# Windowed attention over a narrower set of keys, with latent tokens ordered by grid column

## The chip, the cores and the metric

The kernel runs on 1 core of one Trainium2 chip. The metric is the device time of one execution in microseconds (us); the time before is the median of 3 runs.

## The reference

Two trunk layers act on 640 tokens of width 1024: 512 latent tokens, which lie on a grid of 8 rows by 64 columns, and 128 context tokens. Each layer applies a modulated RMSNorm, one combined q/k/v projection, attention in three groups of heads, an output projection, a second norm, and an expert layer (for each token 8 heads choose 16 of 16384 single-neuron experts). What the change touches is group A, six heads of neighbourhood attention:

```
col_ok = (kcols >= cs_b) & (kcols < cs_b + NA_COLS)        # a window of 16 columns per query
bias = rpb[:, dr_idx][:, :, dc_idx]                        # learned, by row and column distance
s_lat = einsum(q_row, k_blk) * scale + bias
s_lat = where(mask, s_lat, -inf)
s_ctx = einsum(q_row, k_ctx) * scale                       # all 128 cached context keys
p = softmax(concatenate([s_lat, s_ctx]))
o = einsum(p[..., :nk], v_blk) + einsum(p[..., nk:], v_ctx)
```

The window is min(8, rows) rows high, which here is all 8 rows, and 16 columns wide, clamped at the edges: the first column of the window is clip(column - 8, 0, 48). Groups B (4 heads, two softmax maps each) and C (6 query heads on 2 key heads) attend to all latent and all context keys. Context queries see context keys alone.

## The kernel before, in words

Everything stays in SBUF apart from the weights, which stream through a ring of four 512 KB blocks by SyncE's queue (lines 372 to 400), and the experts. Tokens lie in 5 tiles of 128: tiles 0 to 3 are latent, tile 4 is context. A latent tile holds two grid rows, since token = 64 * row + column.

The stages are: modulation from `w_mod` (for layer 0 at the very start, 48 blocks, `mod_tile`, L460), norm, projection, attention, output projection, norm, queries, experts. The two expert stages gather 1280 times in all (5 tiles of 128 slots in each layer), 128 rows of 8 KB each time, by GpSimd's queue (L1310). VectorE takes the dot products (L1252), ScalarE builds a diagonal (L858 to L868), TensorE adds up (L660).

**Attention** (`attention(l)` on each engine) works through the list MAPS, made by `attention_plan`: first group A (3 chunks of 2 heads, each over tiles 0 to 4: 30 maps, 24 of them latent), then B (40 maps), then C (30 maps). A map is one head's softmax over one tile of queries. Per pair of maps:

- TensorE computes the scores of both, 512 latent keys in one matmul (L547), 128 cached context keys in a second (L549), into two PSUM pairs. A context tile has one matmul of 128 keys (L544). It first waits for the exponentials of the pair before, since the two PSUM areas are used again.
- VectorE adds the bias table to the 512 latent scores in PSUM (L1086, group A alone), and takes the negated row maximum over 640 columns (L1087); after the exponential it takes the reciprocal of the sum (L1092).
- ScalarE takes the exponential of 640 columns with its sum (L772) into one of 8 `prob` buffers.
- GpSimd multiplies by the reciprocal (L1346).
- Three maps later TensorE transposes the probabilities, 5 blocks of 128 (L579), and ScalarE copies them from PSUM (L782). Four maps later TensorE multiplies them with the values, 5 blocks for two heads (L564), and ScalarE copies the result (L787).

A float32 matmul shows as two instructions in the trace, so x4 of L547 is two score tiles, x20 of L564 is 5 blocks of 2 heads. Each engine's order is written out by hand in its loop over n; TensorE's is scores of a pair, then values of a unit, then transposes of an item.

**The bias table** is 6 heads by 896 columns on 128 partitions. GpSimd's queue loads it at the head of each layer behind the rotary tables and the cached keys and values (L1319 to L1325), as two DMAs of 64 partitions, each reading 14 of 15 rows of 64 values for each head. Then GpSimd adds the column mask in 6 instructions of 896 columns (L1329). In layer 0 this stands beside the modulation blocks, in layer 1 beside the first norm, where VectorE writes the normed activations (`norm`, L1020, L1022, L1027). VectorE waits for `bias_ready` only at the head of attention.

## Time and profile before

| | us |
|---|---|
| median of 3 runs (lowest, highest) | 5093.67 (5089.64, 5100.22) |
| the profiled execution, its own time | 5083.82 |
| its span, first to last instruction | 5082.0 |
| layer 0: attention, from the last projection tile to the last copy | 318 to 632 |
| layer 1: the same | 2827 to 3141 |

The profile gives one execution: for each engine the busy time, for each idle stretch what ended it, and the chain of work that ended last. PEclk is TensorE's granted clock as a share of full speed (0.50 is the lower of its two levels, 1.2 GHz, and 1.00 the upper, 2.4 GHz). Matmul durations double, nearly, from the one to the other.

### The profile page before, as it was taken

Reading aid. Unit: us, or ns where it says so; the run is one execution under the profiler, and the core shown is the slowest. Engines: PE = TensorE matmul, PEld = TensorE weight load, DVE = VectorE, ACT = ScalarE, POOL = GpSimd, SP = SyncE. Lnnn points to the kernel's source line nnn. Section 1 sums busy time; section 2 is a strip of 40 time slices with the busy share of each in tenths; the row PEclk is TensorE's granted clock in tenths of the full one; section 3 lists DMA queues with packets and bytes.
Section 4 is the critical chain, followed back from the end, with each engine's and each line's share of the span. In section 5 each row is a group of like instructions: output and inputs, shape, how many; then the busy total and the mean of one; then the engine's idle time right before and its main releaser. Section 6 shows DMA issues by size and latency. Waiting matters only on the chain.

```text
span 5082.0 us, 42863 instructions
## 1 busy us (share of the span) xinstructions
PE 3751.2 (74%) x14332; PEld 1733.4 (34%) x14332; DVE 2830.4 (56%) x6026; ACT 1445.8 (28%) x4223; POOL 1400.0 (28%) x1477
## 2 busy tenths in 40 slices
PE   5777779777777777777767776867777777777776
PEld 1464435222222222323234544442222222222222
DVE  2443365564675756754455334557657567576544
ACT  1223422222222222222222334222222222322222
POOL 1011200233343333433320111003333434334332
PEclk8886789899999999999988858989999999999999
DMA  8110012999999999999951000119999999999997
GB/s 277 54 36 1 1 58 91 392 410 414 417 413 420 415 408 410 409 411 380 419 188 47 19 1 14 62 55 410 418 415 412 415 416 409 419 409 416 417 420 294
DMA packets 214077, 1460.21 MB, mean 287 GB/s; under 512 B 23968, under 2 KB 24224, under 8 KB 49248
## 3 DMA queue, kind: packets, MB, share of 16 engines
q0 software_dynamic: 186496, 1355.11, 65.2%
q1 hardware_dynamic: 27360, 102.37, 5.8%
q8 instruction: 113, 1.85, 0.1%
q14 instruction: 108, 0.88, 0.0%
HBM read 1453.19 MB, written 4.19 MB: 287 GB/s over the span
## 4 chain that ended last, share of the span: by engine, by line
PE 39%; DMA 38%; DVE 12%; ACT 6%; issue 4%; POOL 0%; SPq 0%; ACTq 0%; DVEq 0%; POOLq 0%
DMA work<-expert_dram,work 26%; PE psum L660 17%; DMA hT<-expert_dram,work 10%; PE psum L449 10%; DVE work L1252 4%; PE psum L547 3%; PE psum L564 2%; PE psum L579 2%; ACT work L868 2%; PE psum L519 2%; DVE hT L1252 2%; DVE work L992 1%; ACT work L858 1%; DMA ring<-w_mod_dram 1%; ACT work L782 1%
## 5 line engine op out<-in xcount | busy, mean ns | idle before, releaser
L660 PE MATMUL psum<-work 128*128 128x512 f32 x3416 | 1611.7, 616 | 560.3 <-ACT work L868 554.9
L1252 DVE SCALAR_TENSOR_TENSOR work<-work,psum 128x1024 f32<-128x1024 f32 x854 | 1041.5, 1220 | 875.8 <-DMA work<-expert_dram,work 875.4
L1310 POOL DMA_INDIRECT work<-expert_dram,work x854 | 831.6, 974 | 1522.6 <-PE psum L660 1349.9
L660 PEld LDWEIGHTS psum<-work 128*128 128x128 f32 x3416 | 627.9, 193 | 1534.2 <-ACT work L868 885.1
L660 PE MATMUL psum<-hT,work 128*128 128x512 f32 x1704 | 805.7, 617 | 317.7 <-ACT work L868 317.2
L858 ACT ACTIVATE work<-work,xinv 128x2 f32<-128x2 f32 x640 | 189.1, 295 | 2385.2 <-DVE work L1252 1588.6
L1252 DVE SCALAR_TENSOR_TENSOR hT<-hT,psum 128x1024 f32<-128x1024 f32 x426 | 519.5, 1220 | 428.5 <-DMA hT<-expert_dram,work 428.3
L1310 POOL DMA_INDIRECT hT<-expert_dram,work x426 | 413.0, 969 | 834.4 <-PE psum L660 668.4
L660 PEld LDWEIGHTS psum<-hT,work 128*128 128x128 f32 x1704 | 312.8, 193 | 803.4 <-ACT work L868 485.5
L449 PE MATMUL psum<-hT,split 128*128 128x128 f16 (+1 forms) x2880 | 436.2, 313 | 58.3 <-DVE hT L1027 58.3
L868 ACT ACTIVATE work<-const,work 128x128 f32<-128x128 f32 x1280 | 434.1, 386 | 0.0
L449 PEld LDWEIGHTS psum<-hT,split 128*128 128x128 f16 x2880 | 233.2, 101 | 265.0 <-issue 71.7
L862 ACT ACTIVATE work<-work 128x1 f32<-128x1 f32 x1280 | 307.1, 287 | 20.8
L1087 DVE TENSOR_REDUCE stat<-psum 128x1 f32<-128x640 f32 (+1 forms) x200 | 141.0, 710 | 266.5 <-PE psum L549 209.0
L941 DVE SCALAR_TENSOR_TENSOR split<-ring,bscale,split 128x1024 f16<-128x1024 f32 x88 | 112.8, 1282 | 201.0 <-ACT split L701 200.4
L564 PE MATMUL psum<-work 128*64 128x128 f32 x1344 | 122.5, 342 | 122.8 <-ACT work L782 122.8
L772 ACT ACTIVATE work<-psum,stat 128x640 f32<-128x640 f32 (+1 forms) x200 | 141.7, 708 | 239.5 <-DVE stat L1087 238.7
L547 PE MATMUL psum<-work 64*128 64x512 f32 (+1 forms) x320 | 142.6, 983 | 50.3 <-ACT work L772 47.9
L1346 POOL TENSOR_SCALAR work<-work,stat 128x640 f32<-128x640 f32 (+1 forms) x120 | 85.2, 713 | 284.6 <-DVE stat L1092 284.6
L460 PE MATMUL psum<-ring,cT 128*2 128x512 f32 x384 | 107.4, 660 | 58.0 <-DMA ring<-w_mod_dram 49.5
L579 PE MATMUL psum<-const,work 128*128 128x128 f32 x672 | 141.6, 349 | 8.2 <-ACT work L782 8.2
L564 PEld LDWEIGHTS psum<-work 128*64 128x64 f32 x1344 | 97.1, 173 | 145.2 <-ACT work L782 145.2
(152 smaller groups left out, 2744.5 us busy)
## 6 DMA issues: line engine op xcount, KB each, us to landing
ring<-w_mod_dram SPq DMA_DIRECT2D x96, 512.0 KB, 5.6
ring<-w_in_dram SPq DMA_DIRECT2D x40, 512.0 KB, 3.5
ring<-w_query_dram SPq DMA_DIRECT2D x32, 512.0 KB, 3.6
work<-expert_dram,work POOLq DMA_INDIRECT x854, 8.5
ring<-w_out_dram SPq DMA_DIRECT2D x16, 512.0 KB, 3.5
hT<-expert_dram,work POOLq DMA_INDIRECT x426
work<-rpb_dram POOLq DMA_DIRECT2D x4, 1344.0 KB, 19.2
xT<-xT_dram SPq DMA_DIRECT2D x1, 2560.0 KB, 11.7
```

The lines of the kernel that those rows point to most:

```text
L449: last = pe.matmul(out[:, lo:hi_], w[:, i, k, :], x[:, j, k, lo:hi_], start=(s == 0 and n == 0), stop=(s == KC - 1 and n == 2))
L547: pe.matmul(ps[:, 0:NLAT], q, qk[kp:kp + kn, m["k"], 0:NLAT], start=True, stop=True)
L564: last = pe.matmul(psum[64 * hh:64 * hh + 64, 6 + u % 2, 0:P], v, probT[:, u % 2, hh, b * P:(b + 1) * P], start=(b == 0), stop=(b == nb - 1))
L579: last = pe.transpose(pair[2][:, b * P:(b + 1) * P], src[:, b * P:(b + 1) * P], con("ident"))
L660: last = pe.matmul(out[:, cols_], diag[:, n % NDIAG, :], rows[n % NBUF][:, D + 512 * half:D + 512 * half + 512], start=(s == 0), stop=(s = ...
L772: act.activation(prob[:, n % NPROB, 0:w], pair[n % 2][:, 0:w], ACT.Exp, bias=stat[:, 0, n % NPROB:n % NPROB + 1], accum_out=stat[:, 1, n % ...
L858: act.activation(act_out[:, s:s + 2], act_in[:, s:s + 2], ACT.Gelu_apprx_tanh, scale=xinv[:]).then_inc(gelu_done, 1)
L862: act.activation(coef[:, s + k:s + k + 1], act_out[:, s + k:s + k + 1], ACT.Copy, scale=weight[:, t % 2, s + k:s + k + 1]).then_inc(coef_d ...
L868: act.activation(diag[:, (n + k) % NDIAG, :], con("ident"), ACT.Copy, scale=coef[:, s + k:s + k + 1]).then_inc(diag_done, 1)
L1087: dve.tensor_reduce(stat[:, 0, n % NPROB:n % NPROB + 1], ps[:, 0:TOK if lat else NCTX], AX_X, ALU.max, negate=True).then_inc(max_done, 1)
L1252: dve.scalar_tensor_tensor(u, u, 1.0, pair[t % 2], ALU.mult, ALU.mult, accum_out=act_in[:, s:s + 1]).then_inc(dot_done, 1)
L1310: pool.indirect_dma_start(rows[n % NBUF], None, a[f"expert{l}"], bass.IndirectOffsetOnAxis(expert[:, t % 2, s:s + 1], 0)).then_inc(row_in[ ...
```

## The change

The latent tokens are put in the order 8 * column + row, so that a tile of 128 queries is 16 columns of all 8 rows, and a range of keys is a range of columns. The host orders the input, the rotary tables and the output accordingly. For group A the table COL_SPAN gives for each latent tile the first latent key, the number of latent keys and where its columns start in the bias table: 256 keys for tiles 0 and 3, 384 for tiles 1 and 2. Scores, bias add, maximum, exponential, scaling, transposes and the product with the values work on these keys and the 128 of context alone. The bias table is laid out on the host as 896 columns for each head (256 + 384 + 256, of which tiles 1 and 2 use the same 384), and loaded by one DMA of 128 partitions with 5376 values in a row; the mask is 112 columns, each added to 8 neighbouring values. Groups B and C have the same work as before.

```diff
+COL_SPAN = ((0, 256, 0), (0, 384, 256), (128, 384, 256), (256, 256, 640))
...
-          ("iota", 128), ("iota16", 16), ("mask", 64)]
+          ("iota", 128), ("iota16", 16), ("mask", 112)]
...
+def span(m):
+
+    if m["t"] == TT - 1:
+        return NLAT, 0
+    return COL_SPAN[m["t"]][0:2] if m["kind"] == "A" else (0, NLAT)
+
+
+def width(m):
+    return span(m)[1] + NCTX
...
-        bias = at(o, 6, BROWS, GRID_W); o += 6 * BROWS * GRID_W
+        bias = at(o, 6, 896); o += 6 * 896
...
-                                    pe.matmul(ps[:, 0:NLAT], q, qk[kp:kp + kn, m["k"], 0:NLAT], start=True, stop=True)
+                                    at_, nk = span(m)
+                                    pe.matmul(ps[:, 0:nk], q, qk[kp:kp + kn, m["k"], at_:at_ + nk], start=True, stop=True)
...
-                                    last[x] = pe.matmul(ps[:, NLAT:TOK], q, kc[kp:kp + kn, m["cc"], :], start=True,
+                                    nk = span(m)[1]
+                                    last[x] = pe.matmul(ps[:, nk:nk + NCTX], q, kc[kp:kp + kn, m["cc"], :], start=True,
...
-                        nb = TT if it["t"] < TT - 1 else 1
+                        nb = width(it) // P
...
-                                v = vN[:, TT - 1 if nb == 1 else b, vs] if b < TT - 1 else vc[:, vs]
+                                v = vc[:, vs] if nb > 1 and b == nb - 1 else vN[:, span(it)[0] // P + b, vs]
...
-                        for b in range(TT if it["t"] < TT - 1 else 1):
+                        for b in range(width(it) // P):
...
-                        w = TOK if m["t"] < TT - 1 else NCTX
+                        w = width(m)
...
-                            r0 = 6 - 2 * m["t"]
-                            b = bias[:, m["head"], r0:r0 + ROWS, :].rearrange("p r c -> p (r c)")
-                            link(dve.tensor_tensor(ps[:, 0:NLAT], ps[:, 0:NLAT], b, ALU.add))
-                        dve.tensor_reduce(stat[:, 0, n % NPROB:n % NPROB + 1], ps[:, 0:TOK if lat else NCTX], AX_X, ALU.max,
+                            nk, at_ = COL_SPAN[m["t"]][1:3]
+                            b = bias[:, m["head"], at_:at_ + nk]
+                            link(dve.tensor_tensor(ps[:, 0:nk], ps[:, 0:nk], b, ALU.add))
+                        dve.tensor_reduce(stat[:, 0, n % NPROB:n % NPROB + 1], ps[:, 0:width(m)], AX_X, ALU.max,
...
-                for par in range(2):
-                    pool.dma_start(bias[64 * par:64 * par + 64],
-                                   a["rpb"][l, :, :, 1 - par:1 - par + BROWS, :]).then_inc(bias_in, 16)
-                pool.wait_ge(bias_in, 16 * 2 * (l + 1))
+                pool.dma_start(bias, a["rpb"][l]).then_inc(bias_in, 16)
+                pool.wait_ge(bias_in, 16 * (l + 1))
                 for h in range(6):
-                    pool.tensor_tensor(bias[:, h], bias[:, h], con("mask").unsqueeze(1).to_broadcast(
-                        [P, BROWS, 64]), ALU.add).then_inc(bias_ready, 1)
+                    b = bias[:, h].rearrange("p (c r) -> p c r", r=ROWS)
+                    pool.tensor_tensor(b, b, con("mask").unsqueeze(2).to_broadcast([P, 112, ROWS]),
+                                       ALU.add).then_inc(bias_ready, 1)
```

## Rows read from the trace of the kernel before

**Rows 1.** The page: DMA share, in tenths, in 40 equal slices of 127 us.
```profile
DMA  8110012999999999999951000119999999999997
```

**Rows 2.** Windows over both A phases, each layer's; columns are in the first line.
```profile
core 0: us, PE busy (x) PEld busy (x) DVE busy (x) ACT busy (x) POOL busy (x), PEclk, DMA share, GB/s
...
325.40:427.40 102.00, 67.83 (x449) 45.38 (x449) 39.12 (x84) 40.56 (x98) 20.93 (x29) 0.74 0.00 1
2834.20:2936.20 102.00, 67.93 (x449) 45.41 (x449) 39.05 (x84) 40.54 (x98) 20.92 (x29) 0.74 0.00 1
```

**Rows 3.** The chain by line, 325.43 to 427.4 us, layer 0's A phase.
```profile
by line: PE psum L547 19.5%; PE psum L564 19.2%; DVE stat L1087 13.1%; PE psum L579 12.0%; DVE psum L1086 10.5%; ACT work L782 8.9%; issue 7.0%; ACT work L772 5.2%; PE psum L549 4.3%; DVE stat L1092 0.2%; ACTq L771 0.1%
```

**Rows 4.** Groups by form in the same stretch: busy us, mean ns | idle before.
```profile
L1087 DVE TENSOR_REDUCE stat<-psum 128x1 f32<-128x640 f32 x24 | 19.8, 824 | 0.8
L772 ACT ACTIVATE work<-psum,stat 128x640 f32<-128x640 f32 x24 | 19.0, 794 | 44.0 <-DVE stat L1087 43.6
L1086 DVE TENSOR_TENSOR psum<-psum,work 128x512 f32<-128x512 f32 x24 | 16.6, 690 | 46.5 <-PE psum L549 46.5
L782 ACT ACTIVATE work<-psum 128x640 f32<-128x640 f32 x22 | 15.4, 699 | 19.6 <-PE psum L579 19.6
L772 ACT ACTIVATE work<-psum,stat 128x128 f32<-128x128 f32 x6 | 2.2, 366 | 0.0
L1087 DVE TENSOR_REDUCE stat<-psum 128x1 f32<-128x128 f32 x6 | 1.7, 282 | 11.7 <-PE psum L544 11.7
L782 ACT ACTIVATE work<-psum 128x128 f32<-128x128 f32 x4 | 1.1, 272 | 1.9 <-PE psum L579 1.9
```

**Rows 5.** Timeline of TensorE in layer 0's A phase: start us, us, what.
```profile
336.01 2.08 PE L547 MATMUL psum<-work 64*128 64x512 f32 x4 [2.83 <-ACT work L772]
338.45 1.33 PE L579 MATMUL psum<-const,work 128*128 128x128 f32 x5
341.68 2.40 PE L564 MATMUL psum<-work 128*64 128x128 f32 x20 [1.90 <-ACT work L782]
356.88 1.31 PE L564 MATMUL psum<-work 128*64 128x128 f32 x20 [0.79 <-ACT work L782]
358.12 0.77 PE L579 MATMUL psum<-const,work 128*128 128x128 f32 x5
358.82 1.13 PE L547 MATMUL psum<-work 64*128 64x512 f32 x4
```

**Rows 6.** Windows: the bias load at the start, and in layer 1.
```profile
15.00:35.00 20.00, 5.62 (x12) 0.28 (x12) 0.00 (x0) 0.00 (x0) 0.00 (x0) 0.53 1.03 248
2598.00:2601.00 3.00, 3.00 (x9) 1.64 (x8) 0.00 (x0) 0.95 (x2) 0.00 (x0) 0.62 0.99 406
2602.00:2614.00 12.00, 4.61 (x20) 2.61 (x18) 6.42 (x8) 4.23 (x5) 0.00 (x0) 0.85 1.00 200
```

**Rows 7.** The chain in order of time at the start: start us, us, what.
```profile
14.93 21.84 DMA ring<-w_mod_dram
```

**Rows 8.** Timeline of VectorE and GpSimd after layer 1's bias load.
```profile
2616.18 13.56 POOL L1329 TENSOR_TENSOR work<-work,const 128x896 f32<-128x896 f32 x6 [18.76 <-DMA work<-rpb_dram]
2618.25 2.71 DVE L1027 TENSOR_TENSOR hT<-work,hT 128x640 f16<-128x640 f32 x1
2631.91 0.82 DVE L1027 TENSOR_TENSOR hT<-work,hT 128x640 f16<-128x640 f32 x1
```

**Rows 9.** Windows: the first pairs of A, and part of B, layer 0.
```profile
325.40:342.00 16.60, 7.86 (x30) 4.55 (x32) 9.22 (x18) 5.94 (x13) 3.39 (x5) 0.50 0.00 0
460.00:540.00 80.00, 59.02 (x283) 37.62 (x282) 32.50 (x73) 30.94 (x80) 11.78 (x15) 0.50 0.00 1
```

**Rows 10.** Timeline: ends of the first, fourth and fifth expert tile, layer 0.
```profile
1284.88 1.02 ACT L837 ACTIVATE work<-psum 128x1024 f32<-128x1024 f32 x1
2260.74 1.00 ACT L837 ACTIVATE work<-psum 128x1024 f32<-128x1024 f32 x1
2589.74 1.02 ACT L837 ACTIVATE work<-psum 128x1024 f32<-128x1024 f32 x1 [3.50 <-PE psum L660]
```

More of the change, by code:

```diff
@@ L48 @@
 B_SCALE = 32.0 ** -0.5
-BROWS = 14
+COL_SPAN = ((0, 256, 0), (0, 384, 256), (128, 384, 256), (256, 256, 640))
 HEADS, TOPK, NK = 8, 16, 128
@@ L776, in attention @@
                         i = BY_LAST[n - LAG_T]
-                        w = TOK if ITEMS[i]["t"] < TT - 1 else NCTX
+                        w = width(ITEMS[i])
                         act.wait_ge(tr_done, NITEM * l + i + 1)
@@ L1342, in _ @@
                         m = MAPS[n]
-                        w = TOK if m["t"] < TT - 1 else NCTX
+                        w = width(m)
                         s = n % NPROB
@@ L1352, in _, with bias_columns, by_column, by_row @@
                 gather(l)
+def bias_columns():
+    q0 = np.repeat([0, 16, 48], [32, 48, 32])
+    kcol = np.concatenate([np.arange(32), np.arange(48), 32 + np.arange(32)])
+    return q0[None, :] + np.arange(P)[:, None] // ROWS, kcol[None, :]
+def by_column(x):
+    return x.reshape(ROWS, GRID_W, D).transpose(1, 0, 2).reshape(NLAT, D)
+def by_row(x):
+    return x.reshape(GRID_W, ROWS, D).transpose(1, 0, 2).reshape(NLAT, D)
 def constants():
@@ L1371, in constants @@
     c["iota16"] = np.tile(np.arange(16), (P, 1))
-    qc = p[:, None] % GRID_W
-    kcol = np.arange(GRID_W)[None, :]
-    lo = np.clip(qc - 8, 0, GRID_W - 16)
+    qcol, kcol = bias_columns()
+    lo = np.clip(qcol - 8, 0, GRID_W - 16)
     c["mask"] = np.where((kcol >= lo) & (kcol < lo + 16), 0.0, NEG)
@@ L1381, in constants @@
         inv = (np.float32(10000.0) ** (-(np.arange(q, dtype=np.float32)) / np.float32(q))).astype(np.float32)
-        pos = np.where((d // (dim // 2) == 0)[:, None], (tok // GRID_W)[None, :], (tok % GRID_W)[None, :])
+        pos = np.where((d // (dim // 2) == 0)[:, None], (tok % ROWS)[None, :], (tok // ROWS)[None, :])
         ang = pos.astype(np.float32) * inv[d % q][:, None]
@@ L1411 @@
     ins = {}
-    x = np.concatenate([x_sample.reshape(NLAT, D), x_prompt.reshape(NCTX, D)], 0)
+    x = np.concatenate([by_column(x_sample), x_prompt.reshape(NCTX, D)], 0)
     ins["xT"] = x.T.reshape(KC, P, TOK).transpose(1, 0, 2)
@@ L1434 @@
         ins[f"expert{l}"] = np.concatenate([peer_u[l], peer_v[l]], 1)
-    rpb = np.zeros((L, 6, 15, 127), na_rpb.dtype)
-    rpb[..., 63 - 15:63 + 16] = na_rpb
-    ins["rpb"] = np.stack([rpb[..., 63 - q:127 - q] for q in range(GRID_W)], 1)
+    qcol, kcol = bias_columns()
+    dc = np.repeat(np.clip(kcol - qcol, -15, 15) + 15, ROWS, axis=1)
+    dr = np.tile(np.arange(ROWS), 112)[None, :] - np.arange(P)[:, None] % ROWS + ROWS - 1
+    ins["rpb"] = na_rpb[:, :, dr, dc].transpose(0, 2, 1, 3)
     ck = np.concatenate([cache_c_k.reshape(L, NCTX, P), cache_b_k.reshape(L, NCTX, 2 * P),
@@ L1457 @@
     v = r["out_v"]
-    return (y[NLAT:].reshape(1, NCTX, D), y[:NLAT].reshape(1, NLAT, D),
+    return (y[NLAT:].reshape(1, NCTX, D), by_row(y[:NLAT]).reshape(1, NLAT, D),
             kT[..., 384:].reshape(1, L, NCTX, 6, 64), v[..., 0:384].reshape(1, L, NCTX, 6, 64),
```

## The prediction

> **What bounds the kernel now.** I read the page first, for the shape of the whole. The DMA share stands at nine tenths or more for 25 of 40 slices [rows 1]: these are the two expert stages, where the gathers set the pace. The change leaves their number and size alone. It acts in the slices with a DMA share near nothing, where attention runs, so I cut a window out of each layer, from the first bias add to the first score tile of group B [rows 2]. Both last 102 us, with TensorE busy 68 us, VectorE 39 and ScalarE 41, and a DMA share of 0.00. No engine is full, and nothing hides the phase. The chain through it [rows 3] says why: it hands on from scores (L547, L549) to bias add and maximum (L1086, L1087), exponential (L772), copy (L782), values (L564), transposes (L579), and then to the next scores, which wait for the exponentials of the pair before. "Issue", 7.0%, is mostly the second exponential's own run. A shorter piece of any of them shortens the loop.
>
> **The change, part by part.** A latent tile of group A has 256, 384, 384 and 256 latent keys in place of 512, a mean of 320, so 192 columns fewer, and 448 wide instead of 640 with the context. Values and transposes go from 5 blocks to 3, 4, 4, 3: 1.5 fewer. Context tiles, B and C keep their work. Each term is the part of the 102 us that a line has on the chain [rows 3] times the share that it loses.
>
> Scores, L547: 19.5% or 19.9 us. Four instructions of 512 columns take 2.08 us at the lower clock and 1.13 at the upper [rows 5], the difference 0.95 being 4 x 512 columns at one clock against the other. So the columns are 1.90 us of 2.08, and 192 of 512 of that is 0.71, or 34%. Part of the rest also hides behind the L549 pair, and I take 30%: 6.1 us.
> Values, L564: 19.2%, 19.6 us. x20 takes 2.40 or 1.31 us [rows 5], so columns are 2.18 of 2.40; 6 of 20 instructions fewer is 0.65, 27%; I take 5.0 us.
> Transposes, L579: 12.0%, 12.2 us; 1.33 or 0.77 us for five [rows 5], columns 1.12; 1.5 of 5 is 0.34, 25%; I take 2.8 us.
> Maximum, L1087: 824 ns at 640 columns and 282 at 128 [rows 4], 1.06 ns a column, so 0.20 us or 25% of 13.1% (13.4 us): 3.3 us.
> Bias add, L1086: 690 ns [rows 4], one width only; with the slope of the maximum 0.20 us or 29% of 10.7 us: 3.1 us.
> Exponential, L772: 794 and 366 ns [rows 4], 0.84 ns a column, 0.16 us or 20% of about 10.5 us (5.2% and half of "issue" and more): 2.1 us.
> Copy, L782: 699 and 272 ns [rows 4], 0.16 us or 23% of 9.1 us: 2.1 us.
> Sum: 24.5 us for a layer, 49 us for two, as long as TensorE's clock stays at the 0.74 of both phases. GpSimd's scaling gets shorter too, but is behind the chain (21 us of 102 [rows 2]); I cost it at nothing, and nothing comes to depend on it. What is late next is the same loop: TensorE's fixed wait for two exponentials.
>
> The clock is the open cost of this part. TensorE's work falls by about as much as the loop (at the mean of both clocks some 0.5 us of scores, 0.5 of values and 0.5 of transposes a unit, 12 units: 18 of 68 us, beside 24.5 of 102), so its share goes from 0.67 to 0.65 only. But the first pairs, which have scores and transposes alone and a share of 0.47, ran at 0.50, and so did B with a share of 0.74 [rows 9]. If all of A ran at 0.50, the chain's 11 score tiles would be 11 x 2.08, its 11 value groups 11 x 2.40, transposes and L549 some 21 us: 70 us against 56 now, and after the cut about three quarters of those 14 us, 10.7 us a layer. If all ran at 1.00, it would be some 12 us a layer better. Being half way, and with the share nearly unchanged, I take no correction.
> The Trainium skill ("TensorE: Matmul & The Clock Gate", The HAM clock gate) says that the throttled state is the default and that activity releases it. By that rule less work among waits that stay would speak against this change, and the sum would be nearer that of the lower clock; the first pairs agree with it, B with its share of 0.74 does not.
>
> **The bias table's load.** Its bytes are the same 2.75 MB a layer, but as 128 rows of 21504 bytes, where before each of 64 partitions had pieces of 14 x 256 bytes. It is slow now: in layer 1 the queue moves 406 GB/s while the tables before it run, and 200 GB/s with the DMA engines as full while the bias runs [rows 6]. At the start 20 us pass at 248 GB/s with a share of 1.03 [rows 6], and the chain lies on it: 21.84 us of waiting for modulation blocks [rows 7]. If the new form runs like the tables, the same 4.96 MB take 12.2 us at 406: 8 us gained, all on the chain, as everything after waits for these blocks and then for xT. Bounds: nothing (the rate stays at 200), and 10 us. I take 8, since long rows ran at 406 in the same queue.
> In layer 1 it lands 12 us x (1 - 200 / 406), about 6 us, earlier. That matters: GpSimd's six mask adds run 2616.18 to 2629.7, and beside them VectorE's operations on the chain take 2.71 us where 0.82 is normal [rows 8]. There are six such places of about 1.8 us: 10.8 us lost. Six to seven us earlier, about two of the six adds fall under the reciprocal and before the first normed tile at 2613.3, so I take 2 x 1.8 = 3.6 us. Bounds: nothing, if the reciprocal is blocked as well, and 10.8. The mask's new form (112 columns, each repeated over 8 neighbours) has the same 896 elements; no row shows this form, and I take the 2.1 to 2.3 us of one add now.
> The Trainium skill ("SBUF — State Buffer", SBUF: two separate sides) calls the port that VectorE and GpSimd share an exclusive lock for a whole instruction; the 2.71 us agree with that.
> The larger mask is 24.6 KB more of constants, under 0.1 us at the rates above. Issuing one DMA fewer saves 0.7 us on GpSimd's queue, which waits for the landing anyway.
>
> **Sum.** 49 + 8 + 3.6 = 60.6 us. The profiled execution took 5083.8 us, so its like would take 5023. It is 9.9 us below the median of the runs shown, 5093.7; against the median the forecast is 5033.
>
> **Rivals.**
> *The lower clock.* All of A at 0.50 leaves 24.5 - 10.7 = 13.8 us a layer, 27.6 in all; with the load's 11.6 that is 39, so 5055. For it: the first pairs and B. Against it: the share of 0.65. Chance 0.18.
> *The load is no faster.* The bias is slow for another reason than its pieces, such as going to 64 partitions at a time through one queue behind others. Then 49 us remain: 5045. For it: the trace shows the rate, not the cause. Against it: 406 GB/s in the same queue. Chance 0.13.
> *The mask add becomes slow.* This is the case on the other side. If GpSimd handles runs of 8 poorly, each of its six adds blocks VectorE in layer 1's norm for its whole length. One extra us for an add costs 6 us; from 9.5 us extra, 11.6 us an add, it eats the 57 us of the other terms; at 14 us it is 6 x 11.9 - 57 = 14 us slower, 5108, before what it does to layer 0's norm. For it: only that the form is unknown. Against it: five times the price for as many elements. Chance 0.04.
> *It does not do what it says, or not where it counts.* If the narrower tiles did not shorten the loop, since a fixed wait took the place of each cut, the time would be 5094, or up to 11.6 us less with the load's part. Against it: every piece of the chain scales with columns in these rows. Chance 0.02.
> The expert stages gather other rows together. Four tiles took 1304.9 us, 326 us a tile [rows 10]; the last of them took 329.0, 3 us more than that. No row says that the new mix is better or worse. Ten tiles with such differences of their own add some 5 us of spread both ways.
>
> **How the numbers follow.** The forecast case has 0.63, its time is 5033. About 0.2%, or 10 us, is what a measurement of this kernel can tell from no change. The low end is 49 + 8 + 10.8 = 68 off the median, and 8 more if runs fall like the profiled one: 5018. The high end takes in the lower clock with a few us of spread: 5061. Faster takes all cases but the last two, 0.94; slower 0.04; same 0.02.
>
> **What would show it.** In the changed profile: A's windows of 76 to 78 us with a clock near 0.74; the maximum at 0.55 to 0.69 us; x12 and x16 of L564; xT's load issued some 8 us earlier; fewer than six slow operations of VectorE in layer 1's norm. The prediction is wrong if A's windows stay above 88 us, if the clock falls to 0.50 there, if mask adds last over 4 us each, or if the expert tiles differ by more than 5 us each.

## The result and the profile after

The changed kernel takes 5026.79 us, median of 4 runs (5010.99 to 5032.48), beside 5091.66 (5089.57 to 5100.22) for the kernel before: a ratio of 0.9881, with an interval of 0.9852 to 0.9909. It was timed again in a later comparison: 5020.68 us over 6 runs (4995.43 to 5027.24), ratio 0.9859 [0.9832, 0.9885]. So it is faster by 1.2% to 1.4%, about 65 us. The forecast was 5033. The sum came out right; its parts did not, as this section and the next ones show.

The profiled execution took 5023.02 us, of which the span is 5021.2; before, 5083.82 and 5082.0. Cut at the same events in both traces, the 60.8 us of span went like this (us):

| stretch | before | after | difference |
|---|---|---|---|
| start to layer 0's first VectorE operation of attention | 318.4 | 303.5 | -14.9 |
| layer 0: attention, to its last copy | 314.0 | 295.0 | -19.0 |
| of it A | 102.0 | 85.9 | -16.1 |
| of it C, in which nothing was changed | 89.6 | 86.6 | -3.0 |
| layer 0: out-projection and queries | | | -1.4 |
| layer 0: expert stage | 1682.4 | 1672.8 | -9.6 |
| layer 1: norm and projection | 237.4 | 229.9 | -7.5 |
| layer 1: attention (A again 102.0 to 85.9) | 313.7 | 294.9 | -18.8 |
| layer 1: queries | | | +0.6 |
| layer 1: expert stage | 1630.4 | 1638.7 | +8.3 |
| the end | | | +1.5 |

The windows over the two A phases, with the same events at their ends as in [rows 2]. Columns: stretch, its length, then PE, PEld, DVE, ACT and POOL busy (instructions), the granted clock, the DMA share and GB/s.

```profile
310.56:396.48 85.92, 61.55 (x350) 41.81 (x350) 29.50 (x84) 33.27 (x98) 17.18 (x29) 0.58 0.00 1
2781.70:2867.60 85.90, 61.54 (x349) 41.81 (x349) 29.55 (x84) 33.26 (x98) 17.17 (x29) 0.58 0.00 1
```

TensorE has 99 instructions fewer, 350 for 449, and VectorE and ScalarE as many as before but shorter ones. The third number from the end is the surprise: the granted clock fell from 0.74 to 0.58, that is from half way between the two levels (1.2 and 2.4 GHz) to near the lower. TensorE's busy share did not fall: 61.55 of 85.92 is 0.72, where 67.83 of 102.00 was 0.67. But the share isn't independent of the clock: the same instructions last nearly twice as long at the lower level (sixteen value multiplications 1.97 us below, 1.09 at the upper), so a fallen clock by itself raises it.

The chain through the same stretch by line, to lay beside [rows 3] (scores are L559 and L562 now, values L577, transposes L592, bias add L1099, maximum L1100, exponential L785, copy L795):

```profile
by line: PE psum L577 21.6%; PE psum L559 17.4%; PE psum L592 15.0%; DVE stat L1100 11.1%; DVE psum L1099 8.4%; ACT work L795 7.0%; issue 6.5%; PE psum L562 5.6%; ACT work L785 5.4%; PE psum L555 1.7%; DVE stat L1105 0.2%; ACTq L784 0.1%
```

In us of 85.92: scores 15.0 (before 19.9), values 18.6 (19.6), transposes 12.9 (12.2), maximum 9.5 (13.4), bias add 7.2 (10.7), copy 6.0 (9.1). VectorE's pieces and ScalarE's copy fell by more than a quarter. TensorE's values hardly fell and its transposes rose, though more than a fourth of both is gone: each one that is left takes longer.

The groups by form in that stretch, to lay beside [rows 4]:

```profile
L1100 DVE TENSOR_REDUCE stat<-psum 128x1 f32<-128x512 f32 x12 | 8.3, 691 | 0.4
L785 ACT ACTIVATE work<-psum,stat 128x512 f32<-128x512 f32 x12 | 8.2, 687 | 19.4 <-DVE stat L1100 19.1
L795 ACT ACTIVATE work<-psum 128x512 f32<-128x512 f32 x12 | 7.1, 595 | 13.9 <-PE psum L592 13.8
L785 ACT ACTIVATE work<-psum,stat 128x384 f32<-128x384 f32 x12 | 7.0, 580 | 15.8 <-DVE stat L1100 15.8
L1100 DVE TENSOR_REDUCE stat<-psum 128x1 f32<-128x384 f32 x12 | 6.7, 557 | 0.4
L1099 DVE TENSOR_TENSOR psum<-psum,work 128x384 f32<-128x384 f32 x12 | 6.7, 557 | 19.1 <-PE psum L562 19.1
L1099 DVE TENSOR_TENSOR psum<-psum,work 128x256 f32<-128x256 f32 x12 | 5.1, 424 | 20.4 <-PE psum L562 20.4
```

The maximum takes 691 and 557 ns, a mean of 624, where 824 - 192 x 1.06 = 620 was forecast. The bias add takes 557 and 424, a mean of 490, and 690 - 200 = 490 was forecast from another operation's slope. The exponential's mean is 634 for a forecast of 634. What each narrower instruction costs was known; the slopes held.

TensorE's timeline in A, beside [rows 5]:

```profile
335.50 1.97 PE L577 MATMUL psum<-work 128*64 128x128 f32 x16 [0.69 <-ACT work L795]
338.24 1.23 PE L559 MATMUL psum<-work 64*128 64x256 f32 x4
341.90 0.88 PE L577 MATMUL psum<-work 128*64 128x128 f32 x12 [1.72 <-ACT work L795]
343.08 1.65 PE L559 MATMUL psum<-work 64*128 64x384 f32 x4
```

Two levels stand in this view. Sixteen value multiplications at the lower one take 1.97 us, nearly in proportion to the 2.40 for twenty; twelve take 0.88 where the clock is still at the upper level, and 1.55 at the lower. Of the 11 value groups of latent tiles in this stretch, 4 ran wholly at the lower level before (2.40 us for twenty) and 8 do now. The waits for the copy (0.69, 1.72) are still there.

At the start, where the chain waits for the modulation blocks ([rows 6] and [rows 7] before):

```profile
15.00:25.00 10.00, 2.15 (x6) 0.09 (x4) 0.00 (x0) 0.00 (x0) 0.00 (x0) 0.68 1.01 429
...
25.00:35.00 10.00, 8.11 (x28) 1.02 (x28) 0.00 (x0) 1.18 (x2) 9.31 (x6) 0.81 0.92 326
```

```profile
11.95 13.06 DMA ring<-w_mod_dram
```

429 GB/s in place of 248 beside the bias load, and a wait of 13.06 us in place of 21.84. All waits of the chain for w_mod up to xT's issue add up to 23.4 us (5.68, 13.06 and 4.66) in place of 31.7. xT's load is issued at 35.81 us instead of 45.85, 10.0 us earlier, and takes 10.70 us instead of 11.69. Most of what remains of the 14.9 us are shorter waits for later blocks of w_mod and w_in before the first projection.

In layer 1, beside [rows 8]; each row has start, length, engine, line, what, and in brackets the idle time before it and what ended that:

```profile
2563.09 10.99 POOL L1341 TENSOR_TENSOR work<-work,const 128x896 f32<-128x896 f32 x6 [11.43 <-DMA work<-rpb_dram]
2563.83 4.15 DVE L1005 RECIPROCAL work<-work 128x640 f32<-128x640 f32 x1 [0.80 <-ACT work L752]
2568.01 0.89 DVE L1033 TENSOR_TENSOR work<-xT,work 128x640 f32<-128x640 f32 x1
2568.94 3.52 DVE L1035 TENSOR_SCALAR work<-work,affine 128x512 f32<-128x512 f32 x2
...
2572.38 2.37 DVE L1033 TENSOR_TENSOR work<-xT,work 128x640 f32<-128x640 f32 x1
2575.51 0.82 DVE L1040 TENSOR_TENSOR hT<-work,hT 128x640 f16<-128x640 f32 x1
```

The six mask adds run from 2563.09 to 2574, and begin with the reciprocal rather than after it. An add now takes 1.73 us, 2.07 before. The reciprocal beside them takes 4.15 us, as without them, so it neither blocks them nor is blocked. Two operations of the norm are still slow (3.52 for two that take 0.80 in all elsewhere in this view, 2.37 for 0.82): 4.3 us lost, where six places lost 10.8 before.

### The profile page after: what moved, and what is told of

Its sections match the earlier page's. It is cut to its first block, busy times and chain, and to the rows that moved or that the text cites. A ratio compares the mean times of both kernels' runs of the same rounds, so it can differ in the third digit from the quotient of the medians.

```text
span 5021.2 us, 42429 instructions
## 1 busy us (share of the span) xinstructions
PE 3734.6 (74%) x14116; PEld 1727.7 (34%) x14116; DVE 2805.2 (56%) x6026; ACT 1430.2 (28%) x4223; POOL 1386.1 (28%) x1475
## 4 chain that ended last, share of the span: by engine, by line
PE 40%; DMA 37%; DVE 12%; ACT 6%; issue 4%; POOL 0%; SPq 0%; ACTq 0%; DVEq 0%; POOLq 0%
DMA work<-expert_dram,work 21%; PE psum L673 18%; DMA hT<-expert_dram,work 15%; PE psum L460 10%; DVE work L1265 3%; PE psum L559 3%; PE psum L577 2%; DVE hT L1265 2%; PE psum L592 2%; ACT work L881 2%; PE psum L530 2%; DVE work L1005 1%; ACT work L871 1%; PE psum L498 1%; ACT work L795 1%
## 5 line engine op out<-in xcount | busy, mean ns | idle before, releaser
L673 PE MATMUL psum<-hT,work 128*128 128x512 f32 x1704 | 823.0, 628 | 338.8 <-ACT work L881 335.3
L1100 DVE TENSOR_REDUCE stat<-psum 128x1 f32<-128x640 f32 (+3 forms) x200 | 131.5, 662 | 264.8 <-PE psum L562 208.0
L785 ACT ACTIVATE work<-psum,stat 128x640 f32<-128x640 f32 (+3 forms) x200 | 134.0, 670 | 222.7 <-DVE stat L1100 222.0
L577 PE MATMUL psum<-work 128*64 128x128 f32 x1200 | 117.4, 356 | 106.9 <-ACT work L795 106.9
L559 PE MATMUL psum<-work 32*128 32x512 f32 (+3 forms) x320 | 132.0, 917 | 48.2 <-ACT work L785 46.2
L1358 POOL TENSOR_SCALAR work<-work,stat 128x640 f32<-128x640 f32 (+3 forms) x120 | 77.7, 649 | 261.6 <-DVE stat L1105 261.4
L592 PE MATMUL psum<-const,work 128*128 128x128 f32 x600 | 137.1, 365 | 6.2 <-ACT work L795 6.0
L577 PEld LDWEIGHTS psum<-work 128*64 128x64 f32 x1200 | 91.1, 180 | 131.5 <-ACT work L795 131.5
## 6 DMA issues: line engine op xcount, KB each, us to landing
xT<-xT_dram SPq DMA_DIRECT2D x1, 2560.0 KB, 10.7
```

What stands on the lines that cost most here:

```text
L559: pe.matmul(ps[:, 0:nk], q, qk[kp:kp + kn, m["k"], at_:at_ + nk], start=True, stop=True)
L577: last = pe.matmul(psum[64 * hh:64 * hh + 64, 6 + u % 2, 0:P], v, probT[:, u % 2, hh, b * P:(b + 1) * P], start=(b == 0), stop=(b == nb - 1))
L592: last = pe.transpose(pair[2][:, b * P:(b + 1) * P], src[:, b * P:(b + 1) * P], con("ident"))
L673: last = pe.matmul(out[:, cols_], diag[:, n % NDIAG, :], rows[n % NBUF][:, D + 512 * half:D + 512 * half + 512], start=(s == 0), stop=(s = ...
L785: act.activation(prob[:, n % NPROB, 0:w], pair[n % 2][:, 0:w], ACT.Exp, bias=stat[:, 0, n % NPROB:n % NPROB + 1], accum_out=stat[:, 1, n % ...
L1100: dve.tensor_reduce(stat[:, 0, n % NPROB:n % NPROB + 1], ps[:, 0:width(m)], AX_X, ALU.max, negate=True).then_inc(max_done, 1)
```

## The experiments

The theory after the result: the narrower tiles save what the terms say, TensorE's clock takes a third of it back, and the load was slow because it went to 64 partitions at a time. The rivals: the terms were too large and the clock is beside the point; the load was slow because of its 256-byte pieces. Times by stage below are of one profiled execution each, as A / B / C of layer 0.

**The load alone.** The old kernel, with the bias table arranged on the host as 128 rows and loaded by one DMA. Token order, tile widths and the old mask stay.

```
-                for par in range(2):
-                    pool.dma_start(bias[64 * par:64 * par + 64], a["rpb"][l, :, :, 1 - par:1 - par + BROWS, :])...
-                pool.wait_ge(bias_in, 16 * 2 * (l + 1))
+                pool.dma_start(bias, a["rpb"][l]).then_inc(bias_in, 16)
+                pool.wait_ge(bias_in, 16 * (l + 1))
...
```

> The kernel before, with the bias table laid out on the host as 128 rows of 21504 bytes and loaded by one DMA; token order, 512 keys and the old mask stay. My theory (the load alone gives the gain outside attention): layer 0's attention begins near 304 us, as in the changed kernel, against 318.4 before; six mask adds of 2.07 us each, about three of which still block VectorE in layer 1's norm, which gets 4 to 6 us shorter; A's windows stay at 102 us with a clock of 0.74. In all 18 to 21 us less than before. Rival (half of the 15 us at the start came by chance, from how the DMA packets fell): layer 0's attention begins near 310 us, in all 10 to 14 us less.

Measured: 5064.7 us over 10 runs against 5084.49, ratio 0.9964 [0.9943, 0.9984]. The 20 us between the medians are those of the theory, but the interval reaches from 8 to 29 us and doesn't shut out the rival's 10 to 14. Attention begins at 305.6 us, 12.8 earlier than before, and layer 1's time from the reciprocal to attention is 214.3 us (before 218.0, changed kernel 210.9). The load is worth about 16.5 us by these two (12.8 + 3.7), where the forecast had 8 + 3.6. The mask add stays at 2.067 us: its 1.73 belongs to the mask's new form. There was a second finding. The window over A in the first layer:

```profile
312.70:411.10 98.40, 64.58 (x449) 43.49 (x449) 38.99 (x83) 40.75 (x98) 21.05 (x29) 0.77 0.00 1
```

In layer 1 the same 449 instructions took 101.9 us at a clock of 0.74. No instruction differs, and the lower clock goes with 3.5 us more. C, whose work is the same in the kernel before and the changed one, took 84.7 us (0.94) in layer 0 and 89.6 (0.88) in layer 1 of this same profile.

**The width alone.** The changed kernel with every latent tile of A 512 keys wide again. It takes bias and mask from the wrong columns, so its scores aren't the reference's.

```
-COL_SPAN = ((0, 256, 0), (0, 384, 256), (128, 384, 256), (256, 256, 640))
+COL_SPAN = ((0, 512, 0), (0, 512, 128), (0, 512, 256), (0, 512, 384))
```

> The changed kernel with 512 latent keys in every latent tile of group A again; order, load and mask form stay. It takes the bias from the wrong columns of the table, so the scores are not the reference's. Theory (the width alone shortens A, the order costs nothing): A's windows return to 102 us at a clock of 0.74, 16 us more in each layer, and layer 0's attention still begins near 303.5 us. Rival (the order of tokens changed the clock or the loop by itself): A's windows stay over 2 us away from 102, or the clock away from 0.74 by over 0.04.

Measured: 5054.88 us in one run; A is 102.0 us in layer 0 and 101.9 in layer 1, both at 0.74, and B 115.5. Attention begins at 307.9 us, not near 303.5 as expected, which is the spread of the start (below).

```profile
314.90:416.89 101.99, 67.78 (x448) 45.34 (x448) 39.15 (x84) 40.62 (x98) 21.03 (x29) 0.74 0.00 1
```

The old length and the old clock come back with the width, to a tenth, so nothing else of the change (token order, table layout, spans that start at 128) touches A. Width at the clock that each width gets is worth 16.1 us a layer.

**More work for TensorE.** The changed kernel, with eight extra multiplications in float16 ahead of the values of each unit from the third on, where TensorE mostly waits for the copy anyway. Their result goes to a part of the bank that nobody reads.

```
+        fill = const[:, CO["ones"]:CO["ones"] + 256].bitcast(F16)
...
-                        pe.wait_ge(pt_done, NITEM * l + UNITS[u]["last"] + 1)
                         if u >= 2:
                             pe.wait_ge(o_evac, NUNIT * l + u - 1)
+                        for f in range(8 if u >= 2 else 0):
+                            pe.matmul(psum[:, 6 + u % 2, 256:512], fill[:, 0:P], fill[:, P:3 * P], start=True, stop=True)
+                        pe.wait_ge(pt_done, NITEM * l + UNITS[u]["last"] + 1)
```

> The changed kernel, with 8 extra float16 matmuls of 128 x 256 for each attention unit from the third on, into unused PSUM columns, put where TensorE waits for ScalarE's copy before the values. They compute nothing that is used. Theory (A gained 16 us instead of 24.5 because the granted clock fell from 0.74 to 0.58 there): the clock rises to 0.9 or more in A and B, A's windows shrink from 86 to 66 to 74 us, B's 120 us to 85 to 105, in all 40 to 90 us less than the changed kernel. Rival (the missing gain lies in fixed waits, and the clock only followed): the windows stay at 84 us or more in A, or get longer by part of the extra 1.7 us a unit, some 10 to 20 us a phase.

Measured: 4945.48 us, ratio 0.9722 [0.9673, 0.9771] to the kernel before. Windows over A and B:

```profile
313.10:385.30 72.20, 54.50 (x439) 39.27 (x439) 29.51 (x84) 33.16 (x98) 17.27 (x29) 0.82 0.00 1
385.30:478.30 93.00, 71.63 (x500) 47.64 (x499) 45.90 (x99) 43.98 (x113) 15.76 (x20) 0.82 0.00 1
```

89 instructions more in A, and TensorE is busy for 54.5 us rather than 61.6, as the clock is 0.82 rather than 0.58. A is 13.7 us shorter and B, which the change under study doesn't touch, 22.4. The clock stayed below the 0.9 that was expected, the times are within theirs. The rival's 84 us or more did not come: no fixed wait held A at 86 us, and the clock makes up most, if not all, of what was missing. By this pair A costs 13.7 / 0.24, about 57 us for a whole unit of clock, so an estimate of the fall from 0.74 to 0.58 is some 9 us; 24.5 - 9 = 15.5, for 16.1 measured. This price is no constant. The changed kernel's two layers in its second profile (below) give 3.0 us for 0.04, 75 a unit, and the wide tiles with and without the same extra work (below) 11.1 us for 0.12, 93 a unit; by these the fall would be 12 or 15 us. The clock is given to two places, so such small steps are coarse. Between the two nearest profiles of the narrow tiles, 82.9 us at 0.62 and 72.2 at 0.82, a straight line gives 76.5 us at 0.74. That is an estimate, since one of them has the extra work, but it is the forecast's own 76 to 78 us.

**Halves or pieces.** Two kernels for the load. In the first the new rows of 21504 bytes go by two DMAs to 64 partitions each; in the second one DMA goes to 128 partitions, from a source with 15 grid rows of which it takes 14, so that each partition is six pieces of 3.5 KB.

```
-                pool.dma_start(bias, a["rpb"][l]).then_inc(bias_in, 16)
-                pool.wait_ge(bias_in, 16 * (l + 1))
+                for par in range(2):
+                    pool.dma_start(bias[64 * par:64 * par + 64], a["rpb"][l, 64 * par:64 * par + 64]).then_inc(bias_in, 16)
+                pool.wait_ge(bias_in, 16 * 2 * (l + 1))
```

> The changed kernel, with the bias loaded by two DMAs of 64 partitions each, rows of 21504 bytes. Theory (the short pieces of the old source made it slow): the load moves 400 GB/s or more, layer 0's attention begins near 304 us, and layer 1's mask adds start 14 us after the load's issue, as in the changed kernel. Rival (two loads of 64 partitions each use the path only half): 200 to 250 GB/s with a full DMA share while it runs, layer 0's attention begins near 318 us, the adds 20 us after the issue.

```
+        bias4 = at(o, 6, 14, 64)
...
-                pool.dma_start(bias, a["rpb"][l]).then_inc(bias_in, 16)
+                pool.dma_start(bias4, a["rpb"][l, :, :, 0:14, :]).then_inc(bias_in, 16)
...
```

> The changed kernel, its bias loaded by one DMA of 128 partitions, but from an array in which 14 of 15 rows of 64 values are read for each head, as the kernel before read its own. Theory after e4 (what made the old load slow is that each DMA goes to 64 partitions only): rate and times as in the changed kernel, layer 0's attention begins at 303 to 308 us, layer 1's mask adds start about 12 us after the issue. Rival (short pieces cost as well): the load runs at 200 to 300 GB/s, attention begins at 312 us or later, the adds start 16 us or more after the issue.

Measured, halves (5034.04 us in one run): attention begins at 320.5 us, as late as before the change (318.4). At the start, and in layer 1 at the step from the tables to the bias:

```profile
15.00:35.00 20.00, 1.87 (x4) 0.09 (x4) 0.00 (x0) 0.00 (x0) 0.00 (x0) 0.59 1.02 217
```

```profile
2568.00:2571.00 3.00, 3.00 (x12) 1.53 (x11) 0.00 (x0) 1.92 (x3) 0.00 (x0) 0.97 1.01 413
...
2574.00:2577.00 3.00, 1.72 (x9) 1.03 (x7) 1.14 (x6) 1.49 (x2) 0.00 (x0) 1.00 0.91 186
2577.00:2580.00 3.00, 0.00 (x0) 0.00 (x0) 2.20 (x2) 0.74 (x1) 0.00 (x0) 0.74 1.00 215
```

413 GB/s falls to about 200 with the DMA share still near 1.0, and the rows are long ones. Pieces (5035.48 us in one run, so the whole times don't tell the two apart): attention begins at 308.3 us, and the window at the start shows the full rate:

```profile
15.00:25.00 10.00, 2.97 (x10) 0.19 (x8) 0.00 (x0) 0.00 (x0) 0.00 (x0) 0.75 1.02 425
```

The mask adds begin 12.0 us after the issue, as in the changed kernel, and 19 with the halves. So the halves were the cause, and not the pieces. That it is their 64 partitions, and not that there are two DMAs, is argued: the tables, keys and values before them are several DMAs in the same queue, and 413 GB/s are moved there. Two DMAs to all 128 partitions were not run. This is the rival that had 0.13 in the prediction as the reason for "no faster". It was the right cause, yet it did not stop the gain, because the change does away with the halves as well. The old piece of 14 x 256 bytes is 3.5 KB in a row of the source, which is what this kernel reads, and it costs nothing. The Trainium skill ("DMA: Bandwidth & Descriptors", The descriptor swizzle) has engines 0 to 7 write partitions 0 to 63 and 8 to 15 the rest in a transfer to 128. It describes this shape alone, in which partitions 0 to 63 lie behind the even eight of the 16 ports and the rest behind the odd ones. A transfer to one half would by that map reach eight ports, and the rate agrees (217 for 429 GB/s). The DMA share of 1.02 is that of all 16 engines, and how they shared the work isn't shown here.

**Width with the clock held up.** The wide tiles with the eight extra multiplications, to measure the terms with less of the clock in them.

> e2 (512 keys, bias from the wrong columns) with e3's extra matmuls. Theory (at one and the same clock the narrower tiles are worth what my terms say, 24.5 us a layer at 0.74 and a little less at a higher clock): with the clock at 0.8 or more A takes 94 to 98 us, 22 to 25 more than e3's 72.2. Rival (the terms were too large by themselves): A takes 86 to 90 us, 14 to 17 more than e3's, as between the two kernels without extra matmuls.

Measured: 4978.85 us in one run, A 90.9 at 0.86, B 94.8, C 83.8.

```profile
316.60:407.47 90.87, 65.20 (x535) 46.50 (x535) 39.04 (x84) 40.53 (x98) 21.02 (x29) 0.86 0.00 1
```

Against the 72.2 of the narrow one the width is worth 18.7 us. That is between the two expectations; and the clocks differ still (0.86 and 0.82), in favour of the wide one. At 43 us a unit (from the 72.2 at 0.82 to the 67.9 at 0.92 of the last kernel below) the narrow one would take 70.5 at 0.86, which makes the width 20.4 us, an estimate; the terms scaled to that clock are 13.9 x 0.74 / 0.86 + 10.6 = 22.6.

**The extra work at more places.** Eight at each second map, ahead of the wait for the transposed tile, rather than only ahead of the values.

```
+                    later = [u for x, u in UNIT_BY_LAST.items() if x + LAG_V >= n]
+                    if n % 2 and n < NMAP and later and min(later) >= 2:
+                        pe.wait_ge(o_evac, NUNIT * l + min(later) - 1)
+                        for f in range(8):
+                            pe.matmul(psum[:, 6 + min(later) % 2, 256:512], fill[:, 0:P], fill[:, P:3 * P], start=True,
+                                      stop=True)
```

> e3 with the 8 extra matmuls after every second map, which is the same place in A and C, and twice as often in B. Theory (B is still held by the clock, 0.82 in e3): B goes from 93 to 80 to 88 us at a clock of 0.95 or more, A and C stay at 72 and 84, in all 10 to 25 us less than e3. Rival (in B the extra matmuls now stand before work that is due): B's clock rises but its time stays at 91 us or more.

Measured: 4923.76 us, ratio 0.9686 [0.9648, 0.9724]. A is 72.2 at 0.82 as before, B 89.6 at 0.89, C 81.4 at 1.00. B stayed above the 80 to 88 and below the clock of 0.95 that were expected, and below the rival's 91 us; the whole is 22 us less than with the places of before, as expected, though the intervals of the two ratios overlap. The eight fit into the gap: they are followed by idle time.

```profile
348.43 1.04 PE L572 MATMUL psum<-const 128*128 128x256 f16 x8
350.69 0.44 PE L585 MATMUL psum<-work 128*64 128x128 f32 x4 [1.22 <-ACT work L803]
```

**The mask adds after the norm.** The changed kernel, and GpSimd waits for the norm's last tile before it adds the mask.

```
                 pool.wait_ge(bias_in, 16 * (l + 1))
+                pool.wait_ge(hlow_done, KC * (2 * l + 1))
```

> The changed kernel with GpSimd's mask adds held back until the normed activations are written (so they run beside the projection). Theory (three adds still block VectorE in layer 1's norm): the time from layer 1's reciprocal to its attention shrinks by 4 to 5 us. Rival (VectorE's operations in the projection are blocked in turn, on the chain): it shrinks by less than 2 us or grows by up to 10, in both layers.

Measured: 4992.28 us in one run. From the reciprocal to attention in layer 1 it is 204.3 us for 210.9, 6.6 less, of which 4.3 lie between the reciprocal and the first projection (12.6 to 8.3) and in the norm as a whole (its last operation ends 22.9 us after the reciprocal's start, 27.2 in the changed kernel). The adds run from 2582.07, long before the 2763.3 at which attention wants them, and the norm's operations are all at their usual length:

```profile
2563.21 0.83 DVE L1033 TENSOR_TENSOR work<-xT,work 128x640 f32<-128x640 f32 x1
2564.07 0.80 DVE L1035 TENSOR_SCALAR work<-work,affine 128x512 f32<-128x512 f32 x2
2564.79 0.82 DVE L1033 TENSOR_TENSOR work<-xT,work 128x640 f32<-128x640 f32 x1
```

The run lies 31 us below the changed kernel's profiled execution. Beside these 6.6 it has A at 82.9 us (0.62) in layer 1, 3.0 less, and 24 us less in the expert stages (1664.1 and 1623.2), which is their spread, below; attention in layer 0 began 2.1 later. Of the 6.6 the 4.3 are the edit's, as expected. The other 2.3 lie in the projection. Of the two kernels below with the same edit and the same 22.9 one lacks them (206.5 us) and one has them (204.2), so what makes them isn't shown.

**Sixteen at a place.** Twice as many at each place, the first pairs of A included, 24 behind the first scores, and the late mask adds; then the same extra work with wide tiles, without the late mask adds (which lie outside attention).

```
+                    if (n == 0 or n % 2) and n < NMAP and later:
...
+                        for f in range(16 if n else 24):
+                            pe.matmul(psum[:, bank, 256:512], fill[:, 0:P], fill[:, P:3 * P], start=True, stop=True)
...
+                pool.wait_ge(hlow_done, KC * (2 * l + 1))
```

> The changed kernel with 24 extra matmuls behind the first scores and 16 after every second map of attention, and the mask adds held back as in e8. Theory (TensorE's clock is the only thing that kept attention long): the clock is 0.97 or more in A, B and C, A takes 60 to 67 us, B 82 to 88, C 80 to 82, in all 10 to 35 us less than e7. Rival (16 matmuls last longer than the wait that they fill, 2 us): A at 70 us or more in spite of the clock, B above 90.

> e2 (512 keys, bias from the wrong columns) with the 24 and 16 extra matmuls. Both widths now run at nearly the full clock, which prices the narrower tiles alone. Theory (my terms hold at one clock): TensorE's terms, 13.9 us at 0.74, become about 10 us at 1.0, the other engines' 10.6 stay, so A takes 19 to 22 us more than in e9. Rival (part of the missing gain lies in fixed waits): 17 us more or less.

Measured, narrow: 4937.54 us, ratio 0.9727 [0.9704, 0.9749]; A 70.1 (0.95), B 88.3 (1.00), C 84.0 (1.00). The 60 to 67 us expected for A did not come, and the whole is 14 us above eight at a place where 10 to 35 less were expected; the rival had A right (70 or more) and B wrong (above 90). The extra work now lasts longer than the gap, and here the values follow it without a wait:

```profile
341.30 1.91 PE L574 MATMUL psum<-const 128*128 128x256 f16 x16
343.19 0.88 PE L586 MATMUL psum<-work 128*64 128x128 f32 x12
```

Measured, wide: 4980.78 us in one run, A 88.1 at 0.96. The narrow and the wide window:

```profile
316.70:386.79 70.09, 64.21 (x574) 49.06 (x574) 29.52 (x84) 33.21 (x98) 17.18 (x29) 0.95 0.01 1
...
315.20:403.27 88.07, 74.42 (x672) 55.75 (x672) 39.10 (x84) 40.49 (x98) 20.95 (x29) 0.96 0.00 1
```

At nearly the same clock, and nearly the upper one, the width is worth 88.1 - 70.1 = 18.0 us, again between the expectations. Scaled to that clock, the forecast's terms for TensorE (6.1 + 5.0 + 2.8 = 13.9) become 13.9 x 0.74 / 0.96 = 10.7, with the other engines' 10.6 that is 21.3. So they may be too large by a sixth, or the extra work hides a part of the cut; the two aren't told apart here.

**The best of these.** Eight at a place, the first pairs included, 24 at the first scores, late mask adds.

> e9 with 8 extra matmuls at a place in place of 16, so e7's fill, 24 matmuls behind the first scores, and the mask adds held back. Theory (the parts add up): A 68 to 70 us, B 88 to 90, C 81 to 82, layer 1 from its reciprocal to attention 204 to 206 us; median 0 to 15 us below e7's 4924. Rival (e9's median, 14 us above e7's, came from the held-back mask adds rather than from the length of the fill): A, B and C as said, but layer 0's attention begins after 312 us or layer 1's stretch takes 210 us or more.

> The changed kernel once more, for its ratio beside the same chip's runs of the kernel before, and a second profile. Theory (60.6 us less, of which attention 38, the start 10 to 15, layer 1's norm 6 to 7): ratio 0.987 to 0.989; A 85.9, B 115.4, C 86.6 us in both layers, the expert stages of 1660 to 1685 and 1620 to 1655 us without a tie to the token order. Rival (part of the gain came from luckier expert stages): ratio of 0.990 or more.

Measured: 4920.85 us over 5 runs (4909.84 to 4935.67), ratio 0.9677 [0.9653, 0.9702], beside the changed kernel's 5020.68 and the 5086.68 of before in the same comparison. It beats both, by 100 and by 166 us. It is not to be told from the kernel with eight at each second map (4923.76). B takes 87.7 and 88.3 us in its two layers, C 82.9 and 81.4, attention begins at 309.8 us and layer 1's stretch takes 204.2, so the late mask adds did not cost the sixteen their 14 us; the length of the extra work is what is left. Its A window:

```profile
316.60:384.50 67.90, 53.25 (x461) 38.74 (x461) 29.53 (x84) 33.14 (x98) 17.19 (x29) 0.92 0.00 1
```

Its A is 4.3 us shorter than with eight at each second map (72.2 at 0.82), and what differs there is the extra work in the first pairs. The first 16.4 us of A ran at 0.69 with it and at 0.50 without, the rest at 1.00 and at 0.92.

The changed kernel's ratio, 0.9859, lies just below the 0.987 to 0.989 that was expected, and away from the rival's 0.990. In its new profile A was 85.9 us at 0.58 in layer 1 and in layer 0

```profile
309.70:392.63 82.93, 58.20 (x349) 39.39 (x350) 29.52 (x84) 33.27 (x98) 17.19 (x29) 0.62 0.00 1
```

with the same instructions: the second pair in which another clock goes with 3 us.

**The expert stages** of all profiles: layer 0 between 1664 and 1684 us, layer 1 between 1623 and 1652. Their sum is 3312.8 and 3326.9 us in the two kernels with the old order of tokens, and 3287 to 3326 in those with the new one. The first profile's -9.6 and +8.3 are of this spread. A small gain from the new order isn't ruled out by two profiles of the old one.

## Why the prediction was right, step by step

**Attention, 49 us forecast, 37.8 found.** The step that failed is "I take no correction": the clock in A was taken as 0.74, and fell to 0.58. The working argued over the busy share, and even that went the other way than forecast (0.72 found, 0.65 forecast), since the instructions that are left last longer at the lower clock; so the share was no guide. The result, 16.1 us a layer, is nearer the rival of the lower clock, 13.8, than the forecast's 24.5. That rival's evidence, first pairs and B at 0.50 [rows 9], was the better one and deserved more than 0.18. Its price of the clock, 10.7 us for the whole way from 0.74 to 0.50, is somewhat low beside the 9 us or more that the experiments give for two thirds of that way. The windows that were to show the forecast right, 76 to 78 us at 0.74, are 85.9 at 0.58.

**The terms of the cut** held where the clock is the same. The same pair of latent tiles without values before and after, both at the lower clock, takes from the start of its scores to the next ones 6.59 us (from 329.42) and 5.53 us (from 313.27), with 128 keys fewer: 1.06 us. The terms give 1.08 (scores 0.43, four VectorE operations 0.54, exponential 0.11). At 0.74 the straight line between two narrow profiles makes the width 102.0 - 76.5 = 25.5 us, for the forecast's 24.5. At higher clocks, with extra work in both widths, it is less: 20.4 for 22.6, and 18.0 for 21.3, as above. (Two of the forecast's products are slightly off, 30% of 19.9 being 6.0 and not 6.1, and three quarters of 14 being 10.5 and not 10.7; nothing hangs on it.) So the terms fit, as far as this estimate goes, at the clock that they were made for, and the miss of this part is the clock's.

**C and B.** Taken at nothing, since their work is the same. B agrees (115.5 and 115.4). C gave 3.0 and 2.6 us, with the clock at 0.91 for 0.88. That may be luck: C took 84.7 and 89.6 us in the two layers with the load alone, and 86.5 (0.91) and 90.0 (0.86) in the two layers of the kernel with the pieces, whose A and B are those of the changed one. Why C's clock varies isn't shown, and the forecast had no term for it.

**The start, 8 us forecast, 14.9 found.** The term was undersized. xT's load was issued 10.0 us earlier, at the upper bound that was given, and later waits were shorter by 4.9 us more. That second part varies: over the 12 profiles with one DMA to 128 partitions attention began 8.5 to 15.7 us earlier, 10.3 in the middle, so the 10 us of the bound are the typical size and the first profile was a lucky one. All are measured from the 318.4 us of a single profile; the halves had 320.5. The reason given, pieces, was wrong; the halves were the cause.

**Layer 1's norm, 3.6 us forecast, 7.5 found.** The step was "about two of the six adds fall under the reciprocal": three do, since they take 1.73 us each and not 2.07, and the lower bound's condition, a blocked reciprocal, didn't hold. The three that are left cost 4.3 us in place of 10.8, so that 6.5 us are gained there (7.1 from the reciprocal to attention). For the load alone the term was right: it gave 3.7 us with the old mask. What it lacked was the mask's new form, put at the old price: with the halves, so without the faster load, the stretch takes 213.5 us for 218.0.

**The mask add**, the case on the other side: it got faster (1.73 us), so that case fell at its first condition.

**The signs.** The maximum takes 0.56 and 0.69 us, the values come in x12 and x16, and two operations of the norm are slow instead of six, as forecast. Of the signs of being wrong none came, though the clock of 0.58 stopped near the 0.50 that was one.

**Sum.** 49 + 8 + 3.6 = 60.6 forecast; 37.8 + 14.9 + 7.5 = 60.2 found, with 0.6 elsewhere. The total is right because three misses cancel: A gave 17 us less, C 5.6 more, start and norm 11 more. The spread of the expert stages, put at 5 us both ways, is larger: their sums span 40 us, 20 both ways.

## What to carry to other kernels

Before costing a cut in work for TensorE, read the granted clock of its stage, and price both the clock staying and its falling; here, where it was between the levels, less work lowered it (0.74 to 0.58), and the busy share rose all the same. A single figure for the price won't do: it was 43 to 93 us a unit in the pairs above. Where a stage is bound by a chain of waits, unused multiplications placed in gaps that are longer than they are can be worth more than the cut itself (here 100 us more beside 66, some 4 of them from the late mask adds). Some of them placed in the first pairs were worth 4 us in A by themselves. Load all 128 partitions with one DMA rather than two halves, and put GpSimd's bulk work where VectorE isn't on the chain.

## What the runs showed of the hardware that was not expected

The clock: 350 instructions instead of 449 in A brought 0.58 instead of 0.74, at a busy share of 0.72 instead of 0.67; 89 unused ones brought 0.82, and in B 0.53 became 0.82 with a share of 0.77 instead of 0.74. The Trainium skill ("TensorE: Matmul & The Clock Gate", The HAM clock gate) says that throttled is the default and activity releases it. Where multiplications were added to A or B, or taken from A, the clock of that stage moved that way in each of these runs. The busy share doesn't order them: 0.67 had the clock at 0.74, while 0.72 had 0.58 and 0.74 had 0.53.

The same program's A took 98.4 and 101.9 us in its two layers, and 82.9 and 85.9 in another, with the clocks 0.77 and 0.74, and 0.62 and 0.58: a difference of 3 us in such a stage needs its clock beside it.

The DMA share doesn't give the rate: 217 and 429 GB/s both show 1.0.

GpSimd's add of 896 elements takes 2.07 us when the mask is repeated over an index outside its 64 columns, and 1.73 when each element is repeated over eight neighbours. The three that run beside the reciprocal keep their 1.73 us, and it keeps its 4.15.
